# Two PSUM banks for the residual groups, two for the logits, and a first gather that yields transposed rows

## The reference, cut to what matters

```python
x = x + jnp.einsum('bsc,cd->bsd', gate_a * ya + gate_b * yb, w_out[l])
x = x + expert_choice_swiglu(rms_norm(x, norm2_g[l]), w_router[l], w_gate[l], w_up[l], w_down[l])

def expert_choice_swiglu(h, w_router, w_gate, w_up, w_down):
    aff = jax.nn.softmax(jnp.einsum('bsd,de->bse', h, w_router), axis=-1)
    g, idx = lax.top_k(jnp.swapaxes(aff, 1, 2), cap)        # 64 tokens for each of 16 experts
    xin = jax.vmap(lambda hb, ib: hb[ib])(h, idx)
    a = jnp.einsum('becd,edf->becf', xin, w_gate)
    u = jnp.einsum('becd,edf->becf', xin, w_up)
    y = jnp.einsum('becf,efd->becd', jax.nn.silu(a) * u, w_down) * g[..., None]
    # y is added back to the rows idx
```

## Time and profile before

| | us |
|---|---|
| median of 3 runs | 934.76 (934.64 to 937.41) |
| profiled execution, its own time | 935.29 |
| its span, first to last instruction | 933.5 |
| TensorE matmul busy | 877.3 (94% of the span) |
| VectorE, ScalarE busy | 348.1, 248.8 |
| mean DMA rate over the span | 257 GB/s |

### The profile page before, as it was taken

The page is one execution under the profiler, slowest core; times in us unless marked ns, Lnnn a source line. Parts: engine busy times, 40 slices in busy tenths (PEclk is TensorE's granted clock), DMA queues, the critical chain, the costliest instruction groups (busy, mean ns, idle before and its releaser), DMA issues.

```text
span 933.5 us, 11210 instructions
## 1 busy us (share of the span) xinstructions
PE 877.3 (94%) x4710; PEld 557.0 (60%) x4710; DVE 348.1 (37%) x599; ACT 248.8 (27%) x447; POOL 21.8 (2%) x42
## 2 busy tenths in 40 slices
PE   5999899799989999999999999999998999989985
PEld 5999666577868888999834343353434334334332
DVE  4468676765714433332613222213131221221203
ACT  4433766665633232222021010010100001001002
POOL 1040000000000000000000000000000000000001
PEclk8999999999999999999999999999999999999999
DMA  8433111302126623771774999999999999999992
GB/s 263 97 92 91 46 46 46 113 18 72 52 84 204 210 78 96 274 267 53 309 270 181 389 426 427 428 429 428 427 425 429 429 429 427 427 428 427 427 411 99
DMA packets 77920, 239.77 MB, mean 257 GB/s; under 512 B 7728, under 2 KB 63152, under 8 KB 65072
## 3 DMA queue, kind: packets, MB, share of 16 engines
q1 hardware_dynamic: 72304, 235.94, 64.2%
q10 hardware_dynamic: 5568, 3.13, 1.2%
HBM read 236.96 MB, written 2.10 MB: 256 GB/s over the span
## 4 chain that ended last, share of the span: by engine, by line
PE 74%; DMA 19%; DVE 4%; ACT 2%; issue 1%; POOL 0%; SPq 0%; DVEq 0%; ACTq 0%
PE psum L1248 16%; DMA wslot<-in_w_down 14%; PE psum L868 10%; PE psum L870 10%; PE psum L869 10%; PE psum L1282 9%; DMA wslot<-in_w_up 4%; PE psum L1302 3%; PE psum L1005 2%; PE psum L1212 2%; PE psum L874 2%; PE psum L1017 2%; DMA w_raw<-in_w_in 1%; PE psum L975 1%; PE psum L991 1%
## 5 line engine op out<-in xcount | busy, mean ns | idle before, releaser
L1248 PE MATMUL psum<-wslot,xinT 128*64 128x512 f32 x1024 | 232.1, 600 | 12.8 <-DMA wslot<-in_w_up 7.4
L1248 PEld LDWEIGHTS psum<-wslot,xinT 128*64 128x64 f32 x1024 | 71.9, 137 | 155.5 <-issue 140.6
L1282 PE MATMUL psum<-wslot,actT 128*64 128x512 f32 x512 | 112.7, 594 | 5.1 <-DMA wslot<-in_w_down 5.1
L1384 DVE TENSOR_TENSOR w_lo<-w_raw,w_hi 128x1024 fp32r<-128x1024 f32 (+1 forms) x56 | 65.2, 1185 | 75.9 <-ACT w_hi L575 75.5
L868 PE MATMUL psum<-hT_hi,w_hi 128*128 128x512 f32 x224 | 88.9, 397 | 1.4 <-DVE qB_next L1482 1.4
L870 PE MATMUL psum<-hT_hi,w_lo 128*128 128x512 f32 x224 | 87.5, 391 | 0.0
L869 PE MATMUL psum<-hT_lo,w_hi 128*128 128x512 f32 x224 | 87.5, 391 | 0.0
L1282 PEld LDWEIGHTS psum<-wslot,actT 128*64 128x64 f32 x512 | 37.8, 137 | 75.0 <-issue 73.8
L816 ACT ACTIVATE act<-psum 128x512 f32<-128x512 f32 x16 | 9.6, 598 | 211.1 <-PE psum L1248 211.1
L575 ACT ACTIVATE w_hi<-w_raw 128x1024 fp32r<-128x1024 f32 (+1 forms) x56 | 55.9, 1022 | 23.8 <-PE psum L870 18.1
L1709 DVE TENSOR_TENSOR x<-x,psum 128x512 f32<-128x512 f32 x56 | 36.0, 684 | 67.6 <-PE psum L1302 67.6
(11 more groups left out here) (194 smaller groups left out, 1249.0 us busy)
## 6 DMA issues: line engine op xcount, KB each, us to landing
wslot<-in_w_up SPq DMA_DIRECT2D x32, 2048.0 KB, 28.7
wslot<-in_w_gate SPq DMA_DIRECT2D x31, 2048.0 KB, 24.5
wslot<-in_w_down SPq DMA_DIRECT2D x31, 2048.0 KB, 32.2
w_raw<-in_w_in SPq DMA_DIRECT2D x40, 512.0 KB, 4.6
w_raw<-in_w_out SPq DMA_DIRECT2D x8, 512.0 KB, 7.7
x_in<-in_x SPq DMA_DIRECT2D x4, 512.0 KB, 10.3
w_raw<-in_w_o_a SPq DMA_DIRECT2D x8, 256.0 KB, 2.9
x<-in_x SPq DMA_DIRECT2D x1, 2048.0 KB, 7.8
```

What stands on the lines that cost most here:

```text
L1248: mm = pe.matmul(bank[2 * e + n][CAP * f:CAP * f + CAP, :], xinT[:, HALF * h + k, CAP * e:CAP * e + CAP], wslot[slot][:, k, SEQ * f:SEQ * ...
L1282: mm = pe.matmul(bank[4 + f][CAP * e:CAP * e + CAP, :], actT[:, e, k, CAP * h:CAP * h + CAP], wslot[slot][:, k, SEQ * f:SEQ * f + SEQ], st ...
L1384: dve.tensor_tensor(lo, raw, hi.bitcast(F32), ALU.subtract).then_inc(w_split, 1)
```

## The change

Residual groups use banks 0 and 1 in turn; logits use 2, 3, 2, 3, and the wait of `route` on the adds goes, with one on the earlier logits' read in its place. For the first pair VectorE builds `pick_first` instead of `pick`: slots equal to place, times `rstd`, 8 operations of 128x64. TensorE then takes columns of `x2` (every fourth, 128 of them) as the stationary operand and `pick_first` as the moving one, 16 matmuls of 128x128 for each half, which gives transposed and scaled rows. Half 0 goes to four banks and is read by four VectorE operations of 128x128, each followed by its own signal; half 1 goes to bank 6 and is read at once. `xin_first`, `slot_rstd`, the ScalarE reads and the transposes of the first pair are gone; `make_pick(0)`, one operation, comes after the reads of half 0.

```diff
@@ -306,8 +304,8 @@
         bank_of += [3, 5, 3, 5, 3, 5] + [6, 6, 0, 1, 2, 3] + [6, 6] + [i % 4 for i in range(2 * KC - 2)]
-        bank_of += [i % 4 for i in range(D // P // 2 * NT)]
-        logit_bank = (0, 1, 2, 4)
+        bank_of += [i % 2 for i in range(D // P // 2 * NT)]
+        logit_bank = (2, 3, 2, 3)
         by_act = [g[0] in ("tok", "gate") for g in groups]
@@ -392,9 +390,11 @@
                 eng.wait_ge(added, 8 * (PAIRS - 1) + f + 1)
-        def xin_of(p):
-
-            return xin_next if p else xin_first
+        first_banks = [bank[i] for i in (2, 3, 6, 7)]
+
+        def wait_xin(eng, p, h):
+
+            eng.wait_ge(xin_done, HALF - 1 + 2 * p + h + 1)
         def wait_split(eng, n):
...
@@ -831,8 +828,6 @@
                                     scale=slot_aff[:, p % 2:p % 2 + 1]).then_inc(y_hi_done, 1)
-            read_xin(0, 0)
-            read_xin(0, 1)
             for p in range(PAIRS):
@@ -1119,8 +1114,8 @@
                 pe.wait_ge(h2T_dve_done, c + 1 + (k0 > 0))
-                if c < NT - 1:
-                    pe.wait_ge(proj_read_dve, N_COL + N_RES - NT + c + 1)
+                if c >= 2:
+                    pe.wait_ge(smax_done, c - 1)
                 for k in range(k0, k1):
@@ -1177,7 +1172,7 @@
             def gather_slots(p, into):
-                pe.wait_ge(pick_done, NT + p)
+                pe.wait_ge(pick_done, p + 1)
                 if p:
@@ -1185,20 +1180,12 @@
                 mm.then_inc(slots_gathered, 1)
-            def gather_first(f):
-
-                cols = slice(SEQ * f, SEQ * f + SEQ)
-                for c in range(NT):
-                    stat = pick[:, c, :, :].bitcast(F32)
-                    if f == 0:
-                        pe.wait_ge(pick_done, c + 1)
-                        mm = pe.matmul(bank[0][:, 0:1], stat, rstd[:, c:c + 1],
-                                       start=(c == 0), stop=(c == NT - 1), skip_group_check=True)
-                        if c == NT - 1:
-                            mm.then_inc(rstd_gathered, 1)
-                    mm = pe.matmul(bank[6 + f][:, :], stat, x2[:, c, cols],
-                                   start=(c == 0), stop=(c == NT - 1), skip_group_check=True)
-                mm.then_inc(gathered, 1)
+            def gather_first(h, c, k):
+
+                rows = x2[:, c, SEQ * h:SEQ * h + SEQ].rearrange("p (i k) -> p k i", k=HALF)
+                into = first_banks[k][:, 0:P] if h == 0 else bank[6][:, P * k:P * k + P]
+                return pe.matmul(into, rows[:, k, :], pick_first[:, c, :, :], start=(c == 0), stop=(c == NT - 1),
+                                 skip_group_check=True)
             def gather(p, f):
@@ -1215,8 +1202,8 @@
             def turn_xin(p, f):
-                pe.wait_ge(xin_read, 2 * p + f + 1)
-                rows = xin_of(p)[:, SEQ * f:SEQ * f + SEQ].rearrange("p (i k) -> p k i", k=HALF)
+                pe.wait_ge(xin_read, 2 * (p - 1) + f + 1)
+                rows = xin_next[:, SEQ * f:SEQ * f + SEQ].rearrange("p (i k) -> p k i", k=HALF)
                 for k in range(HALF):
@@ -1232,7 +1219,8 @@
                 for h in range(2):
-                    pe.wait_ge(xin_done, 2 * p + h + 1)
+                    if p or h:
+                        wait_xin(pe, p, h)
                     if h == 0 and p:
@@ -1244,6 +1232,8 @@
                         for k in range(HALF):
+                            if m == 0:
+                                pe.wait_ge(xin_done, k + 1)
                             for f in range(2):
@@ -1295,7 +1285,7 @@
                     if c == 0 and p + 1 < PAIRS:
-                        pe.wait_ge(xin_done, 2 * (p + 1) + f + 1)
+                        wait_xin(pe, p + 1, f)
                     elif c or p:
@@ -1303,11 +1293,14 @@
                     mm.then_inc(scattered, 1)
-            keep_clock(4)
-            gather_first(0)
             keep_clock(3)
-            turn_xin(0, 0)
-            keep_clock(3)
+            for c in range(NT):
+                pe.wait_ge(pick_first_done, 2 * c + 2)
+                for k in range(HALF):
+                    mm = gather_first(0, c, k)
+                    if c == NT - 1:
+                        mm.then_inc(gathered, 1)
+            keep_clock(1)
             for p in range(PAIRS):
@@ -1316,9 +1309,11 @@
                     if step == 5:
-                        gather_first(1)
+                        for k in range(HALF):
+                            for c in range(NT):
+                                mm = gather_first(1, c, k)
+                        mm.then_inc(gathered, 1)
                     if step == 7:
-                        turn_xin(0, 1)
                         gather_slots(0, bank[5])
@@ -1647,23 +1642,29 @@
             dve.wait_ge(pos_done, 1)
-            def make_pick(p, tiles):
-
-                n = tiles[-1] + 1 - tiles[0]
-                part = slice(tiles[0], tiles[-1] + 1)
-                wide = [P, n, 2, CAP]
+            def make_pick_first(c, e):
+
+                dve.tensor_scalar(pick_first[:, c, e, :], slot_id[:, :], pos[:, c, e:e + 1], rstd[:, c:c + 1],
+                                  ALU.is_equal, ALU.mult).then_inc(pick_first_done, 1)
+
+            def make_pick(p):
+
+                wide = [P, NT, 2, CAP]
                 place = slot_id[:, :].unsqueeze(1).unsqueeze(1).to_broadcast(wide)
-                own = pos[:, part, 2 * p:2 * p + 2].unsqueeze(3).to_broadcast(wide)
+                own = pos[:, :, 2 * p:2 * p + 2].unsqueeze(3).to_broadcast(wide)
                 if p:
                     dve.wait_ge(give_turned, p)
-                dve.tensor_tensor(pick[:, part, :, :], place, own, ALU.is_equal).then_inc(pick_done, 1)
+                dve.tensor_tensor(pick[:, :, :, :], place, own, ALU.is_equal).then_inc(pick_done, 1)
             def read_turned_xin(p, f):
-                dve.wait_ge(xin_turned, 2 * p + f + 1)
+                if p:
+                    dve.wait_ge(xin_turned, 2 * (p - 1) + f + 1)
+                else:
+                    dve.wait_ge(gathered, HALF + 1)
                 gain = g2_rows[:, HALF * f:HALF * f + HALF].unsqueeze(2).to_broadcast([P, HALF, P])
                 dve.tensor_tensor(xinT[:, HALF * f:HALF * f + HALF, :],
-                                  bank[6 + f][:, :].rearrange("p (k i) -> p k i", i=P), gain, ALU.mult)\
+                                  bank[6 + f if p else 6][:, :].rearrange("p (k i) -> p k i", i=P), gain, ALU.mult)\
                     .then_inc(xin_done, 1)
@@ -1709,16 +1710,19 @@
             for c in range(NT):
-                make_pick(0, [c])
-            dve.wait_ge(rstd_gathered, 1)
-            dve.tensor_copy(slot_rstd[:, 0:1], bank[0][:, 0:1]).then_inc(slot_rstd_done, 1)
-            for f in range(2):
-                read_turned_xin(0, f)
+                for e in range(2):
+                    make_pick_first(c, e)
+            for k in range(HALF):
+                dve.wait_ge(gathered, k + 1)
+                dve.tensor_scalar(xinT[:, k, :], first_banks[k][:, 0:P], g2_rows[:, k:k + 1], None, ALU.mult)\
+                    .then_inc(xin_done, 1)
+            make_pick(0)
+            read_turned_xin(0, 1)
             for p in range(PAIRS):
                 if p + 1 < PAIRS:
-                    make_pick(p + 1, range(NT))
+                    make_pick(p + 1)
                 activate(2 * p)
```

More of the change, by code:

```diff
@@ L168, in encoder_block @@
     act = sb("act", [2, SEQ], 105.5)
-    xin_first = sb("xin_first", [D], 105.5)
+    pick_first = sb("pick_first", [NT, 2, CAP], 102)
     xin_next = sb("xin_next", [D], 48)
     slot_aff = sb("slot_aff", [2], 111.25)
-    slot_rstd = sb("slot_rstd", [1], 111.25 + 1 / 32)
     gf = sb("gf", [D], 100)
@@ L282, in encoder_block @@
         actT_done = sem("actT_done")
-        rstd_gathered = sem("rstd_gathered")
+        pick_first_done = sem("pick_first_done")
         slots_gathered = sem("slots_gathered")
-        slot_rstd_done = sem("slot_rstd_done")
         slot_aff_done = sem("slot_aff_done")
@@ L798, in read_xin @@
             def read_xin(p, f):
-                act_.wait_ge(gathered, 2 * p + f + 1)
+                act_.wait_ge(gathered, HALF - 1 + 2 * p + f + 1)
                 cols = slice(SEQ * f, SEQ * f + SEQ)
[L802 to L805, removed]
+                act_.activation(xin_next[:, cols], bank[6 + f][:, :], ACT.Copy).then_inc(xin_read, 1)
             def high_xn(c):
```

## The result

The changed kernel took 939.29 us as the median of 22 runs (936.25 to 940.62), the kernel before 935.23 us (934.33 to 938.2, 22 runs as well). The ratio is 1.0029, with a 95% interval of 1.0019 to 1.0039: slower by 1.8 to 3.6 us, where 3.15 us less was forecast. The runs of either kernel lie in two groups some 2.5 us apart (934.3 to 935.4 and 937.1 to 938.2 before; 936.3 to 937.2 and 938.3 to 940.6 after). More of the later kernel's runs lie in its upper group, so the ratio of the medians alone, 1.0043, overstates the difference; group against group it is 2.3 us.

What follows compares the result with a forecast made beforehand. TensorE's work up to the first pair's `down` was taken to bound the kernel. Residual stage -0.15, half 0 -2.85, half 1 -0.15 summed to -3.15 us: 932.14 for the profiled execution, 931.6 as the median, range 929.7 to 934.8.

Steps and rivals of the forecast that it cites:

- What bounds the kernel: TensorE's time from 379 us to the first pair's `down` sets the weight stream's start at 514.07; the end follows at a constant.
- The rival in which nothing arrives: Weight stream held by something other than the freed place, so the gain misses the end: 934.8 us, chance 0.08.
- The residual groups: Two banks for four: one TensorE stall of 1.65 us at the third group, behind the DMA that fills `x2`.
- the margin of 0.07 us: Seventh residual group comes at 398.95, the fifth group's add is ready at 398.88, so no further wait.
- The logits: In the router, three waits of `route` on the adds go: gain 1.8 us, residual stage in all -0.15 us.
- The first gather: First pair's gather at 0.117 us a record: half 0 -2.85 us, half 1 -0.15 us.
- The bound "from above": In the first gather, 0.21 us, a strided weight load's duration, as the distance between records if nothing hid it.
- The third rival: Strided loads of the first gather not hidden, 64 records 0.21 us apart: 937.6 us; decides from 0.166 us; chance 0.07.
- The rule quoted beside it: Trainium skill: an access going to another 16-byte line each time pays a penalty; `x2` is read in 16-byte steps.
- a row of transposes: Strided transposes of `xin_next` follow each other like plain ones to 0.005 us, though loads last 0.21 against 0.14 us.
- The first rival: TensorE's clock keeps 2.4 GHz where it fell between 420.90 and 423.90 us: -1.5 us more, 930.1 us, chance 0.28.
- the second rival: Clock falls once more, after the new stall at 385.8 or at another router step: +1.5 us, 933.1 us, chance 0.10.

Runs made afterwards that it cites:

- e3: Changed kernel with each stationary operand of the first gather taken as 128 neighbouring columns of x2, first pair's rows permuted against its weights: 931.32 us, ratio 0.9949.
- e6: Changed kernel with neighbouring stationary columns, first pair's gate and up weights laid out to match, first twelve residual groups on four banks: 929.43 us, ratio 0.9925.
- e8: Changed kernel with neighbouring stationary columns and first pair's gate and up weights laid out to match, two residual banks throughout: 929.75 us, ratio 0.9939.
- e7: Changed kernel with the first twelve residual groups back on four banks, the last four on banks 0 and 1, gather left strided: 937.06 us, ratio 1.001.
- e1: Kernel before with only the new banks for residual groups and logits and the new waits of route, first gather as before: 933.99 us, ratio 0.9979.
- e2: Changed kernel with the banks and logit waits of before, so the new first gather alone: 940.75 us, ratio 1.0061.

## Why the prediction was wrong

What bounds the kernel: right. TensorE's time up to the first pair's `down` sets the start of the stream, and the stream the end. The stretch from that load to the end of the span is the same to 0.4 us in both traces, and it is 419.4 us in e3 and 418.9 in e6 too, whose streams start at 510.43 and 508.58: what a faster gather saves arrives at the end. The rival in which nothing arrives falls.

The residual groups: right in place and size. One stall, 1.51 us for 1.65, behind the DMA that fills `x2`; nothing at the seventh group in the changed kernel, and 0.18 us in e8, so the margin of 0.07 us that I had worked out there was as thin as it looks; e7 took the stall away for 1.8 us.

The logits: right in mechanism, short in size. 1.8 us of waits went; a `route` of 1.69 instead of 1.93 us was not in my sum, and e1 measured -1 to -3 us, and not -0.15.

The first gather: this step failed. "I take 0.117, that of the idle matmuls, and also of the strided transposes" took the distance between loads from an operation that was near in shape and step and still not the same. It measured 0.24 us, twice over 32 records: 64 x 0.123 = 7.9 us more, which turns -3.15 into +4.7; less 0.7 us for `route` that is +4.0, and the 1.5 us of the earlier trace rows, if the executions before have that fall as a rule, bring it to +2.5. Measured was +2.7; that the fall is the rule is not shown. The bound "from above", 0.21, was none either: it was the duration of a transposed load, and a real one lasts 0.329 us and comes every 0.24. The rest of this step held: e3, with the distance as I had it, reaches the expert matmul 4.6 us behind the picks for 4.5.

The third rival was the outcome, in its mechanism, place and point of decision (0.166 us), with 0.07 of the chances; its price was some 2 us short, since it put 0.21 for 0.24 us. The rule quoted beside it spoke against the change, and I weighed a row of transposes higher. Its price would have been the one term that mattered, 64 times.

The clock: in the traces it fell once more or once less at places far from the change (from 12 to 15 us on until about 22 in all nine that could be read, near 180 in seven of them, near 790 in three, near 857 in one, at 421 and 776 only in the one of the kernel before; the last microseconds, where TensorE has no matmuls left, are not counted). Falls behind 530 us cost nothing that shows, as the stream from memory sets the end. The first rival, no fall at 421, is what all traces but that of before show, with the wait on the adds (e2) as without it; so a fall there belongs to the execution as much as to the kernel, as far as these traces tell. A new fall behind the stall at 385.8, the second rival, is in none of them.

## What to carry to other kernels

Before data are read in place as a stationary operand to save a transpose, look at the step between its columns: float32 in steps of 16 bytes or more took twice as long from one load to the next, and in steps of 8 bytes as long as side by side. An operation of the same shape in another mode (here a transpose) is not evidence for this one: the transposes of this case followed each other at half the distance of the real matmuls. Where weights come from memory anyway, as they did here at no cost that showed (e8), choose their layout so that the activations can be read side by side. And a ring of PSUM banks may be cut where its readers keep up, not where a DMA holds the first of them back.

## What I had not expected of the hardware

Float32 loads of 128 stationary columns: 192 ns long and 0.12 us apart side by side, 329 ns and 0.24 us apart in steps of 16 bytes; the same loads for transposes 141 and 209 ns long, 0.112 and 0.117 us apart. Sixteen small matmuls of `route` took 1.69 us straight behind other matmuls and 1.93 us behind a wait. The clock stood at half for 3 us in different places from one execution to the next, with the same operations ahead of them (near 180 us after, not before).
